# The out projection of a fused diffusion layer as seven block products per 256 tokens

## The chip, the cores and the metric

One core of one Trainium2 chip runs the whole program. The metric is the device time of one execution in microseconds; the median of three runs is given. Times inside the program come from one execution taken by the hardware profiler, counted from its first instruction.

## The reference, cut to what matters

The layer runs over 2,048 latent and 256 context tokens (2,304 in all) of 1,024 channels. Two branches (gated linear attention and a Fourier mixer) are each projected to 1,024 channels and merged by gates; what is changed is the last step:

```python
merged = jax.nn.sigmoid(mg_a) * y_a + jax.nn.sigmoid(mg_b) * y_b
x = x + gate[:, None] * (merged @ w_out)
...
y_prompt = _rmsnorm(hp, final_norm_g)
y_sample = _rmsnorm(hs, final_norm_g)
```

`merged` is 2304 x 1024, `w_out` is 1024 x 1024, and everything is float32. Each float32 product is made on TensorE from two roundings, `hi = round(x)` and `lo = x - hi`, as three matmuls: hi·hi, hi·lo and lo·hi.

## The kernel before, in words

The program is written for five engines by hand; every order is the order of the program text, and engines wait for each other's semaphores. The end of the program has three parts.

- **First branch's projection** (`second_branch`, 40 tiles) writes `meb_dram`.
- **Second branch's projection**: 40 tiles, tile `m` being output channels `j = m % 8` of token block `b = m // 8` (four blocks of 512 tokens and one of 256). Per tile TensorE makes 24 matmuls (L2554), DVE multiplies the bank by the gates (L2090), GpSimd adds the other branch (L1166), and SyncE stores the merged tile to `me_dram` (L948). SyncE is also the only queue for the loads.
- **Out projection** (`out_tiles`): nine blocks (`NM`) of `MB` = 256 tokens. A block is four output quarters (token half `u` by channel half `h`, 128 x 512 each) in four PSUM banks; a quarter is eight `k` steps of three matmuls of 512 columns (L2506 is the helper's line). So a block is 96 matmuls, and the nine are 864.

Around it, per block: one load `me_ld` of 1 MB (L970), its rounding on ScalarE (`me_hi`, L1504) and its remainder on DVE (`me_lo`, L1994), each one instruction over 128 x 2048; DVE scales each quarter by the gate row (L2114); GpSimd adds the residual `x_in` per 128 tokens, one instruction over 128 x 1024 (L1173, for the last block L1180); ScalarE squares and sums (L1583) and forms the root (L1585, L1587); DVE scales the rows (L2118; for the last block L2142 and L2147); SyncE stores. `w_out` is loaded in eight pieces, rounded by `high_ow` and finished by `low_ow` during the last blocks of the second branch. The gate rows are made once by two DVE adds (L2102).

## Time and profile before

| | us |
|---|---|
| median of three runs (1958.39 to 1962.95) | 1958.52 |
| span of the profiled execution, first to last instruction | 1959.3 |
| first to last matmul of the out projection | 1756.25 to 1952.34 |
| PE busy, whole span | 1914.4 |
| DVE, ACT, POOL busy, whole span | 1039.4, 876.2, 573.5 |

PE is TensorE's matmuls, PEld its weight loads, DVE is VectorE, ACT is ScalarE, POOL is GpSimd, SP is SyncE. The span of the profiled execution is 0.8 us above the median of the runs; no time outside the span is listed for it. A busy time of PE counts overlapping matmuls once. In the rows, "idle before" is the time that the engine stood still ahead of the instruction, with what released it.

### The profile page before, as it was taken

Reading aid. Unit: us, or ns where it says so; the run is one execution under the profiler, and the core shown is the slowest. Engines: PE = TensorE matmul, PEld = TensorE weight load, DVE = VectorE, ACT = ScalarE, POOL = GpSimd, SP = SyncE. Lnnn points to the kernel's source line nnn. Section 1 sums busy time; section 2 is a strip of 40 time slices with the busy share of each in tenths; the row PEclk is TensorE's granted clock in tenths of the full one; section 3 lists DMA queues with packets and bytes.
Section 4 is the critical chain, followed back from the end, with each engine's and each line's share of the span. In section 5 each row is a group of like instructions: output and inputs, shape, how many; then the busy total and the mean of one; then the engine's idle time right before and its main releaser. Section 6 shows DMA issues by size and latency. Waiting matters only on the chain.

```text
span 1959.3 us, 29951 instructions
## 1 busy us (share of the span) xinstructions
PE 1914.4 (98%) x10453; PEld 1763.4 (90%) x10453; DVE 1039.4 (53%) x1932; ACT 876.2 (45%) x1855; POOL 573.5 (29%) x645
## 2 busy tenths in 40 slices
PE   7899999999999999999999999999999999999998
PEld 2899999999999999999999987888888888898887
DVE  4978787784444435644444545666665322333333
ACT  3565667653445545443545325777732011112222
POOL 0136643053333412335432000002840033331122
PEclk9999999999999999999999999999999999999999
DMA  6578778967788889777888968666438666564333
GB/s 283 207 270 298 278 291 301 380 247 248 245 279 282 260 319 322 245 245 251 280 269 280 356 216 329 233 231 237 177 127 274 225 208 213 189 221 157 132 128 129
DMA packets 166827, 483.17 MB, mean 247 GB/s; under 512 B 14689, under 2 KB 51995, under 8 KB 157725
## 3 DMA queue, kind: packets, MB, share of 16 engines
q1 hardware_dynamic: 152860, 430.99, 63.7%
q10 hardware_dynamic: 13824, 50.34, 6.4%
q8 instruction: 83, 1.36, 0.3%
q14 instruction: 60, 0.48, 0.1%
HBM read 316.64 MB, written 155.20 MB: 241 GB/s over the span
## 4 chain that ended last, share of the span: by engine, by line
PE 72%; DMA 2%; DVE 2%; POOL 2%; ACT 1%; issue 1%; SPq 0%; DVEq 0%; ACTq 0%
PE bank L2219 34%; PE bank L2554 10%; PE bank L2506 10%; PE bank L2519 5%; PE bank L2383 3%; PE bank L2350 2%; PE bank L2448 2%; PE bank L2361 1%; PE bank L2372 1%; POOL h_lo L1038 1%; DMA qd<-qk_dec 1%; DMA x_st<-in_x 1%; PE bank L2391 1%; PE bank L2433 1%; DMA v_ld<-v_dram 1%
## 5 line engine op out<-in xcount | busy, mean ns | idle before, releaser
L2219 PE MATMUL bank<-h_hi,w_op 128*128 128x384 f32 x4032 | 1053.2, 337 | 14.3 <-DVE h_lo L1667 3.4
L2219 PEld LDWEIGHTS bank<-h_hi,w_op 128*128 128x128 f32 x4032 | 733.3, 189 | 20.1 <-issue 19.1
L2219 PE MATMUL bank<-h_lo,w_op 128*128 128x384 f32 x2016 | 675.9, 335 | 0.0
L2219 PEld LDWEIGHTS bank<-h_lo,w_op 128*128 128x128 f32 x2016 | 380.5, 189 | 0.0
L1661 DVE TENSOR_TENSOR w_op<-w_raw,w_op 128x512 fp32r<-128x512 f32 x240 | 190.0, 792 | 96.4 <-ACT w_op L1211 93.0
L1211 ACT ACTIVATE w_op<-w_raw 128x512 fp32r<-128x512 f32 x240 | 149.4, 624 | 160.4 <-PE bank L2219 155.9
L1063 POOL TENSOR_TENSOR decs<-decs,qk_s 128x192 f32<-128x192 f32 x192 | 123.7, 682 | 332.5 <-ACT decs L1285 332.2
L2554 PE MATMUL bank<-in_a,pwa 128*128 128x512 f32 (+1 forms) x960 | 197.3, 368 | 0.0
L2554 PEld LDWEIGHTS bank<-in_a,pwa 128*128 128x128 f32 x960 | 167.3, 189 | 30.0
L2506 PE MATMUL bank<-ow,me_hi 128*128 128x512 f32 x576 | 177.4, 389 | 0.0
L1716 DVE TENSOR_TENSOR outs<-bank,u 128x384 f32<-128x384 f32 x180 | 99.4, 552 | 100.4 <-PE bank L2219 99.5
L1166 POOL TENSOR_TENSOR me_st<-mg_a 128x512 f32<-128x512 f32 (+1 forms) x40 | 63.8, 1598 | 223.3 <-DVE mg_a L2090 223.3
L2506 PEld LDWEIGHTS bank<-ow,me_hi 128*128 128x128 f32 x576 | 107.9, 188 | 22.7 <-DVE me_lo L1994 0.2
L2506 PE MATMUL bank<-ow,me_lo 128*128 128x512 f32 x288 | 112.1, 389 | 0.0
L1048 POOL TENSOR_TENSOR swap<-swap,rope 128x192 f32<-128x192 f32 x96 | 61.1, 667 | 160.7 <-DMA swap<-qk_s 160.7
L1096 POOL TENSOR_TENSOR he<-uf 128x1023 f32<-128x1023 f32 (+2 forms) x7 | 18.7, 2666 | 285.4 <-DMA uf<-u_dram 285.4
L2519 PE MATMUL bank<-in_b,pwb 128*128 128x512 f32 (+1 forms) x480 | 99.3, 368 | 1.8 <-DVE in_b L1994 1.8
L2519 PEld LDWEIGHTS bank<-in_b,pwb 128*128 128x128 f32 x480 | 83.5, 189 | 17.5 <-DVE in_b L1994 2.7
L2090 DVE TENSOR_TENSOR mg_a<-bank,mg_a 128x512 f32<-128x512 f32 (+1 forms) x40 | 25.4, 637 | 136.8 <-PE bank L2554 136.8
L1716 DVE TENSOR_TENSOR u<-bank,p 128x384 f32<-128x384 f32 x72 | 39.9, 554 | 107.4 <-PE bank L2219 107.4
L2350 PE MATMUL bank<-v_ld,kin 128*128 128x256 f32 x272 | 83.3, 390 | 5.9 <-DMA v_ld<-v_dram 4.5
L1173 POOL TENSOR_TENSOR yt<-yt,x_in 128x1024 f32<-128x1024 f32 x16 | 38.1, 2398 | 140.0 <-DVE yt L2114 140.0
(244 smaller groups left out, 2622.2 us busy)
## 6 DMA issues: line engine op xcount, KB each, us to landing
w_op<-wt_dram SPq DMA_DIRECT2D x192, 512.0 KB, 5.6
wt_dram<-w_op ACTq DMA_DIRECT2D x96, 512.0 KB, 4.4
w_raw<-in_w_in SPq DMA_DIRECT2D x48, 768.0 KB, 6.1
w_raw<-in_w_in SPq DMA_DIRECT2D x24, 1024.0 KB, 6.7
qk_dec<-decs SPq DMA_DIRECT2D x48, 384.0 KB, 6.8
mg_dram<-outs SPq DMA_DIRECT2D x24, 768.0 KB, 6.9
swap<-qk_s SPq DMA_DIRECT2D x48, 192.0 KB, 5.8
v_dram<-outs SPq DMA_DIRECT2D x24, 384.0 KB, 4.7
```

Of the source, the lines that this page charges most:

```text
L1048: pool.tensor_tensor(swap[:, q], swap[:, q], rope[:, 1, q], ALU.mult)
L1063: ins = pool.tensor_tensor(e[:, q], e[:, q], qk_s[h % 2][:, x, q], ALU.mult)
L1166: pool.tensor_tensor(me_st[s][:, 0:n], mg_a[s][:, 0, 0:n], mg_a[s][:, 1, 0:n], ALU.add).then_inc(s_me, 1)
L1211: act.activation(w_op[m % RING][:, 0, :, :], w_part(n, j), ACT.Copy).then_inc(s_whi, 1)
L1661: dve.tensor_tensor(op[:, 1, :, :], w_part(n, j), op[:, 0, :, :].bitcast(F32), ALU.subtract).then_inc(s_wlo, 1)
L1716: dve.tensor_tensor(out, group_bank(n, g), other, ALU.add).then_inc(s_d, 1)
L2219: ins = pe.matmul(bnk, w_op[slot][:, part, k, :], h[:, j, k, :], start=(first and k == 0 and part == 0 and h is h_hi), stop=(k == HK - 1 a ...
L2350: pe.matmul(bank[4 + g % 2][:, 0:DV], kin[:, g % 2, :], v_ld[head % 2][:, chunk_at(head, x), :], start=True, stop=True).then_inc(s_ds, 1)
L2383: ins = pe.matmul(out, st, mv, start=False, stop=d == reads[-1])
L2506: ins = pe.matmul(out, st[a], mv[b], start=(k == 0 and p == 0), stop=(k == count - 1 and p == 2))
L2519: ins = pe.matmul(tile_bank(m)[:, 0:n], st[x], mv[y], start=(first and i == 0 and p == 0), stop=(final and i == len(ks) - 1 and p == 2))
L2554: ins = pe.matmul(out, pwa[j][x][:, k, :], in_a[b % 2][y][:, k, 0:n], start=(k == 0 and p == 0), stop=(k == KT - 1 and p == 2))
```

## The change

The 256-token product is made as a 2 x 2 block product with seven products instead of eight (Winograd's form of Strassen's scheme). With A the tokens' half by the channels' half (`a11` to `a22`, out of `me_ld`), and B the same of `w_out` (`b11`, `b21`, `b22`, `b12`):

- TensorE makes seven products of 4 `k` steps x 3 matmuls x 512 columns (`out_product`). Products 4, 5 and 6 add onto the banks of products 0, 2 and 3.
- Weights: `sum_ow` makes three sums and differences of the weight blocks (four instructions), and `high_ow` and `low_ow` now split seven operands of 128 x 2048 instead of eight of 128 x 1024. They stand in the second branch, from its third block to its last, and three `low_ow` stand behind it.
- Tokens: GpSimd makes four sums per block (`sum_me`, 128 x 512); ScalarE and DVE split seven operands of 128 x 512 each (`high_me`, `low_me`) in place of one of 128 x 2048.
- Results: ScalarE copies product 0 and one quarter out of PSUM (`copy_product`, `copy_quarter`); DVE makes five additions of 128 x 512 per block, each with one operand in PSUM (`add_quarter`). The scaling by the gate row moves from DVE to GpSimd, which now makes two instructions of 128 x 1024 per 128 tokens (`finish_rows`: multiply, then add the residual). The last block is finished in halves.
- The load of the gate rows, the norm's weights and the first `x_in` moves behind the last store of the merged tiles; the load of `pwa[7]` comes earlier. `yt` has two sets of buffers, the operands `me_op` have one. The block loop is written out instead of looped.

The diff, cut to its core (the placements in memory, the split of the last block of the second branch into `in_a_end`, and the final block's ScalarE part are left out; ACT copies from `out_bank(b, 0)`, `squares_of` is the old root code for 128 tokens, and the ACT order per block `b` is copy product 0, `squares_of(b - 1, 0)`, `high_me(b + 1, 0)`, `squares_of(b - 1, 1)`, `high_me` of operands 2, 1, 3 and 4, copy the quarter, `high_me` of 5 and 6):

```diff
             return bank[BANK_ORDER[n % 8]]
 
-        def out_bank(slot, u, h):
-            return bank[BANK_ORDER[4 * slot + 2 * u + h]]
+        def out_bank(b, g):
+            return bank[BANK_ORDER[4 * (b % 2) + g]][:, :]
+
+        def me_part(j):
+
+            a11, a12, a21, a22 = (me_ld[:, HK * c:HK * c + HK, P * r:P * r + P] for r in range(2) for c in range(2))
+            return (a11, me_s2[:, :, :], me_s1[:, :, :], a21, a12, me_s2[:, :, :], a22)[j]
+
+        def in_a_of(b, q):
+            return in_a_end[q] if b == NB - 1 else in_a[b % 2][q]
+
+        def in_a_raw_of(b):
+            return in_a_end_raw if b == NB - 1 else in_a_raw[b % 2]
+
+        FINAL = NM - 1
+        ME_ORDER = (0, 2, 1, 3, 4, 5, 6)
+        ME_MADE = (0, 2, 1, 3, 4, 5, 6)
+
+        def summed(b, n):
+
+            return 4 * NP + 4 * b + n + 1
+
+        def me_made(b, what):
+
+            return len(ME_MADE) * b + ME_MADE.index(what) + 1
+
 
...
+            def load_x(b, u):
+                sp.dma_start(x_in[:, u, :], io["x"][(2 * b + u) * P:(2 * b + u + 1) * P, :]).then_inc(s_xin[u], 16)
+
+            for r in range(2):
+                sp.dma_start(res_gate[:, r, :], gate_dram[r:r + 1].to_broadcast([P, D])).then_inc(s_rows, 16)
+            sp.dma_start(gate_b[:, :], io["b_gate"].to_broadcast([P, D])).then_inc(s_rows, 16)
+            sp.dma_start(fng[:, :], io["final_norm_g"].to_broadcast([P, D])).then_inc(s_rows, 16)
+            sp.wait_ge(s_y, 2 * NTILE)
+            for u in range(2):
+                load_x(0, u)
             for s in range(4):
                 sp.wait_ge(s_mest[s], 16 * (GATES_B[s] + NTILE // 4))
 
-            def out_block(b, final):
-
-                if not final:
-                    sp.wait_ge(s_ml, b + 1)
+            def store_y(b, u):
+                if b:
+                    sp.wait_ge(s_yst[u], 16 * b)
+                sp.wait_ge(s_yn, 2 * b + u + 1)
+                sp.dma_start(io["y"][(2 * b + u) * P:(2 * b + u + 1) * P, :], yt[b % 2][u][:, :]).then_inc(s_yst[u], 16)
+
+            for b in range(NM):
+                if b < FINAL:
+                    sp.wait_ge(s_ml, me_made(b, 6))
                     load_me(b + 1)
-                for u in range(2):
-                    if not final:
-                        sp.wait_ge(s_add, 2 * b + u + 1)
-                        sp.dma_start(x_in[:, u, :], io["x"][bass.ds((2 * b + u + 2) * P, P), :]).then_inc(s_xin[u], 16)
-                for u in range(2):
-                    if final and u:
-                        for h in range(2):
-                            sl = slice(512 * h, 512 * h + 512)
-                            sp.wait_ge(s_yn, 2 * b + 2 + h)
-                            sp.dma_start(io["y"][(2 * b + 1) * P:(2 * b + 2) * P, sl], yt[:, 1, sl]).then_inc(s_yst[1], 16)
-                        return
-                    sp.wait_ge(s_yn, 2 * b + u + 1)
-                    y = io["y"][bass.ds((2 * b + u) * P, P), :] if not final else io["y"][(2 * b + u) * P:(2 * b + u + 1) * P, :]
-                    sp.dma_start(y, yt[:, u, :]).then_inc(s_yst[u], 16)
...
+            def sum_me(b, n):
+
+                a11, a12, a21, a22 = (me_part(j) for j in (0, 4, 3, 6))
+                s1, s2 = me_s1[:, :, :], me_s2[:, :, :]
+                out, x, y, op = ((s1, a21, a22, ALU.add), (s2, s1, a11, ALU.subtract), (a21, a21, a11, ALU.subtract),
+                                 (s2, a12, s2, ALU.subtract))[n]
+                if n == 0:
+                    pool.wait_ge(s_mel, 16 * (b + 1))
+                    if b:
+                        pool.wait_ge(s_ml, me_made(b - 1, 6))
+                elif n == 3:
+                    pool.wait_ge(s_ml, me_made(b, 1))
+                else:
+                    pool.wait_ge(s_s, summed(b, 0))
+                pool.tensor_tensor(out, x, y, op).then_inc(s_s, 1)
+
             for m in range(NTILE):
                 b, j, t0, n = tile(m)
                 s = m % 4
@@ -1164,20 +1202,40 @@
                     pool.wait_ge(s_mest[s], 16 * (GATES_B[s] + m // 4))
                 pool.wait_ge(s_yg, NTILE + m + 1)
                 pool.tensor_tensor(me_st[s][:, 0:n], mg_a[s][:, 0, 0:n], mg_a[s][:, 1, 0:n], ALU.add).then_inc(s_me, 1)
-
-
-            def add_block(b):
+                if m == NTILE - 7:
+                    for i in range(3):
+                        sum_me(0, i)
+                elif m == NTILE - 3:
+                    sum_me(0, 3)
+
+
+            def finish_rows(b, u, sl, nth):
+
+                y = yt[b % 2][u][:, sl]
+                pool.tensor_tensor(y, y, res_gate[:, int(b == FINAL), sl], ALU.mult).then_inc(s_add, 1)
+                pool.wait_ge(s_add, nth)
+                pool.wait_ge(s_xin[u], 16 * (b + 1))
+                return pool.tensor_tensor(y, y, x_in[:, u, sl], ALU.add)
+
+            for n in range(3):
+                sum_me(1, n)
+            pool.wait_ge(s_gate, 1)
+            for b in range(FINAL):
+                sum_me(b + 1, 3)
                 for u in range(2):
-                    pool.wait_ge(s_xin[u], 16 * (b + 1))
-                    pool.wait_ge(s_og3, 2 * b + u + 1)
-                    pool.tensor_tensor(yt[:, u, :], yt[:, u, :], x_in[:, u, :], ALU.add).then_inc(s_add, 1)
-
-            with pool.Fori(0, NM // 2) as i:
-                for u in range(2):
-                    add_block(2 * i + u)
-            pool.wait_ge(s_xin[0], 16 * NM)
-            pool.wait_ge(s_og3, 2 * NM - 1)
-            pool.tensor_tensor(yt[:, 0, :], yt[:, 0, :], x_in[:, 0, :], ALU.add).then_inc(s_add, 1)
+                    if u == 0:
+                        pool.wait_ge(s_copied, 2 * b + 2)
+                    pool.wait_ge(s_ad, 5 * b + 4 + u)
+                    finish_rows(b, u, slice(0, D), 2 * (2 * b + u) + 1).then_inc(s_add, 1)
+                if b + 2 <= FINAL:
+                    for n in range(3):
+                        sum_me(b + 2, n)
+            pool.wait_ge(s_ad, 5 * FINAL + 3)
+            finish_rows(FINAL, 1, slice(512, D), 4 * FINAL + 1).then_inc(s_add, 1)
+            pool.wait_ge(s_copied, 2 * NM)
+            finish_rows(FINAL, 0, slice(0, 512), 4 * FINAL + 3).then_inc(s_add, 1)
+            pool.wait_ge(s_ad, 5 * FINAL + 4)
+            finish_rows(FINAL, 0, slice(512, D), 4 * FINAL + 5).then_inc(s_add, 1)
 
...
+            def high_ow(j):
+                if j in (1, 2, 3, 6):
+                    act.wait_ge(s_owl, {1: 3, 2: 1, 3: 2, 6: 4}[j])
+                if j in (0, 4, 5):
+                    act.wait_ge(s_wr[{0: 0, 4: 1, 5: 2}[j]], 48)
+                act.wait_ge(s_y, NTILE + 24 if j == 0 else NTILE + 32 + j)
+                act.activation(ow_op[j][0][:, :, :], ow_src[OW_PART[j]][:, :, :], ACT.Copy).then_inc(s_owh, 1)
+
+            def high_me(b, j):
+                act.wait_ge(s_mel, 16 * (b + 1))
+                if j in (1, 2, 3, 5):
+                    act.wait_ge(s_s, summed(b, {1: 1, 2: 0, 3: 2, 5: 3}[j]))
+                if b:
+                    act.wait_ge(s_out, NPROD * (b - 1) + j + 1)
+                elif j >= 5:
+                    act.wait_ge(s_y, 2 * NTILE)
+                act.activation(me_op[j][:, 0, :, :], me_part(j), ACT.Copy).then_inc(s_mh, 1)
 
             for b in range(NB):
...
+            def sum_ow(n):
+
+                b11, b21, b22, b12, t1, t2, t4 = (ow_src[name][:, :, :] for name in ("b11", "b21", "b22", "b12", "t1", "t2", "t4"))
+                out, x, y = ((t1, b12, b11), (b12, b12, b22), (t2, b22, t1), (t4, b21, t2))[n]
+                for k in ((3, 0), (2,), (), (1,))[n]:
+                    dve.wait_ge(s_wr[k], 48)
+                if n:
+                    dve.wait_ge(s_owl, n)
+                else:
+                    for s in range(GATE_SLOTS):
+                        dve.wait_ge(s_mest[s], 16 * GATES_B[s])
+                if n == 3:
+                    dve.wait_ge(s_y, NTILE + 24)
+                dve.tensor_tensor(out, x, y, ALU.subtract).then_inc(s_owl, 1)
+
+            def low_ow(j):
+                dve.wait_ge(s_owl, 4)
+                low(ow_op[j][1][:, :, :], ow_src[OW_PART[j]][:, :, :], ow_op[j][0][:, :, :], s_owh, j + 1, s_owl)
+
+            def low_me(b, j):
+                low(me_op[j][:, 1, :, :], me_part(j), me_op[j][:, 0, :, :], s_mh, NPROD * b + ME_ORDER.index(j) + 1, s_ml)
 
             for m in range(NTILE):
...
-                    low_ow(j - 4)
+                if b == 0 and j == 1:
+                    low(pwa[7][1][:, :, :], pwa_raw[7][:, :, :], pwa[7][0][:, :, :], s_pwh, 7 + 8, s_pwl)
+                if b == NB - 3 and j >= 5:
+                    sum_ow(j - 5)
+                elif b == NB - 2:
+                    if j == 0:
+                        sum_ow(3)
+                    elif j == 6:
+                        low_ow(0)
                 elif b == NB - 1:
                     if j == 1:
-                        low(me_lo[0][:, :, :], me_ld[:, :, :], me_hi[0][:, :, :], s_mh, 1, s_ml)
-                    elif 3 <= j < 7:
-                        low_ow(j + 1)
-            dve.wait_ge(s_rows, 16 * (8 + 4))
-            for r in range(2):
-                ins = dve.tensor_tensor(res_gate[:, r, :], res_gate[:, r, :], gate_b[:, :], ALU.add)
-            ins.then_inc(s_gate, 1)
-            dve.wait_ge(s_gate, 1)
...
+            def add_quarter(b, step):
+
+                y = yt[b % 2]
+                out, g, other, product = ((u2o[:, :], 1, p1o[:, :], 1), (u4o[:, :], 2, u2o[:, :], 2),
+                                          (y[1][:, 512:D], 3, u4o[:, :], 3), (y[0][:, 512:D], 2, u2o[:, :], 5),
+                                          (y[1][:, 0:512], 3, u2o[:, :], 6))[step]
+                if step == 0:
+                    dve.wait_ge(s_copied, 2 * b + 1)
+                if b + step:
+                    dve.wait_ge(s_ad, 5 * b + min(step, 2))
+                if step in (2, 3):
+                    if b > 1:
+                        dve.wait_ge(s_yst[1 if step == 2 else 0], 16 * (b - 1))
+                    elif b == 0:
+                        for s in range(4):
+                            dve.wait_ge(s_mest[s], 16 * (GATES_B[s] + NTILE // 4))
+                dve.wait_ge(s_out, NPROD * b + product + 1)
+                dve.tensor_tensor(out, out_bank(b, g), other, ALU.add).then_inc(s_ad, 1)
+
+            def scale_rows(b, u):
+                dve.wait_ge(s_rt3, 3 * (2 * b + u + 1) + (b == FINAL))
+                y = yt[b % 2][u][:, :]
+                dve.scalar_tensor_tensor(y, y, rms3[:, u, 1:2], fng[:, :], ALU.mult, ALU.mult).then_inc(s_yn, 1)
+
+            for b in range(NM):
+                if b:
+                    add_quarter(b - 1, 4)
+                    low_me(b, 6)
+                add_quarter(b, 0)
+                if b == 0:
+                    low_ow(5)
+                    low_me(0, 5)
+                    low_me(0, 6)
+                else:
+                    scale_rows(b - 1, 0)
+                add_quarter(b, 1)
+                if b == 0:
+                    low_ow(6)
+                    dve.wait_ge(s_rows, 16 * (8 + 4))
+                    for r in range(2):
+                        ins = dve.tensor_tensor(res_gate[:, r, :], res_gate[:, r, :], gate_b[:, :], ALU.add)
+                    ins.then_inc(s_gate, 1)
+                add_quarter(b, 2)
+                if b:
+                    scale_rows(b - 1, 1)
+                if b < FINAL:
+                    for j in (0, 2, 1):
+                        low_me(b + 1, j)
+                    for j in (3, 4):
+                        low_me(b + 1, j)
+                add_quarter(b, 3)
+                if b < FINAL:
+                    low_me(b + 1, 5)
+
+            sl, y = slice(0, 512), yt[FINAL % 2][1]
+            dve.wait_ge(s_ad, 5 * FINAL + 4)
+            dve.tensor_tensor(u4o[:, :], u2o[:, :], res_gate[:, 1, sl], ALU.mult).then_inc(s_ad, 1)
+            dve.wait_ge(s_ad, 5 * FINAL + 5)
+            dve.wait_ge(s_xin[1], 16 * NM)
+            dve.tensor_tensor(u4o[:, :], u4o[:, :], x_in[:, 1, sl], ALU.add).then_inc(s_ad, 1)
+            dve.wait_ge(s_ad, 5 * FINAL + 6)
+            dve.wait_ge(s_out, NPROD * NM)
+            dve.tensor_tensor(y[:, sl], out_bank(FINAL, 3), res_gate[:, 1, sl], ALU.mult).then_inc(s_ad, 1)
+            dve.wait_ge(s_ad, 5 * FINAL + 7)
+            dve.tensor_tensor(y[:, sl], y[:, sl], u4o[:, :], ALU.add).then_inc(s_ad, 1)
+            scale_rows(FINAL, 0)
+            dve.wait_ge(s_rt3, 6 * FINAL + 8)
             for h in range(2):
                 sl = slice(512 * h, 512 * h + 512)
-                ins = dve.tensor_tensor(yt[:, 0, sl], out_bank(0, 0, h)[:, :], res_gate[:, 1, sl], ALU.mult)
-            ins.then_inc(s_og3, 1)
-            dve.wait_ge(s_xin[1], 16 * NM)
-            scale_half(0)
...
+            def out_product(b, j):
+                bnk = out_bank(b, GROUP[j])
+                if b == 0:
+                    pe.wait_ge(s_owl, 4 + j + 1)
+                pe.wait_ge(s_ml, me_made(b, j))
+                if j < 4:
+                    if b < 2:
+                        pe.wait_ge(s_yg, 2 * NTILE - 8 + 4 * b + GROUP[j] + 1)
+                    elif j == 0:
+                        pe.wait_ge(s_copied, 2 * (b - 1))
+                    else:
+                        pe.wait_ge(s_ad, 5 * (b - 2) + (1, 4, 5)[j - 1])
+                elif j == 4:
+                    pe.wait_ge(s_copied, 2 * b + 1)
+                else:
+                    pe.wait_ge(s_ad, 5 * b + j - 3)
+                first = j < 4
+                for k in range(HK):
+                    for part, w in ((0, 0), (0, 1), (1, 0)):
+                        ins = pe.matmul(bnk, me_op[j][:, part, k, :], ow_op[j][w][:, k, :],
+                                        start=(first and k == 0 and part == w == 0), stop=(k == HK - 1 and part == 1),
+                                        skip_group_check=not first)
+                ins.then_inc(s_out, 1)
+
+            for b in range(NM):
+                for j in range(NPROD):
+                    out_product(b, j)
     return nc
 
```

## Rows read from the trace of the kernel before

**Rows 1.** The page: busy time of each engine, and the chain that ended last
```profile
PE 1914.4 (98%) x10453; PEld 1763.4 (90%) x10453; DVE 1039.4 (53%) x1932; ACT 876.2 (45%) x1855; POOL 573.5 (29%) x645
...
PE 72%; DMA 2%; DVE 2%; POOL 2%; ACT 1%; issue 1%; SPq 0%; DVEq 0%; ACTq 0%
PE bank L2219 34%; PE bank L2554 10%; PE bank L2506 10%; PE bank L2519 5%; PE bank L2383 3%; PE bank L2350 2%; PE bank L2448 2%; PE bank L2361 1%; PE bank L2372 1%; POOL h_lo L1038 1%; DMA qd<-qk_dec 1%; DMA x_st<-in_x 1%; PE bank L2391 1%; PE bank L2433 1%; DMA v_ld<-v_dram 1%
```

**Rows 2.** One stretch inside the out projection: window, length, busy us (instructions), clock, DMA
```profile
1900.00:1920.00 20.00, 20.00 (x90) 16.49 (x89) 7.58 (x7) 5.03 (x9) 4.76 (x2) 1.00 0.36 122
```

**Rows 3.** Timeline at the out projection's first and last matmuls and last DVE pair
```profile
1756.25 0.63 PE L2506 MATMUL bank<-ow,me_hi 128*128 128x512 f32 x2
...
1951.95 0.39 PE L2506 MATMUL bank<-ow,me_lo 128*128 128x512 f32 x1
...
1955.39 1.41 DVE L2147 SCALAR_TENSOR_TENSOR yt<-yt,rms,fng 128x512 f32<-128x512 f32 x2 [1.59 <-ACT rms L1571]
```

**Rows 4.** Groups by line and form from 1500 us on: busy us, mean ns, idle before
```profile
L1166 POOL TENSOR_TENSOR me_st<-mg_a 128x512 f32<-128x512 f32 x32 | 54.2, 1694 | 210.3 <-DVE mg_a L2090 210.3
...
L1994 DVE TENSOR_TENSOR me_lo<-me_ld,me_hi 128x2048 fp32r<-128x2048 f32 x9 | 20.6, 2292 | 85.6 <-ACT me_hi L1504 85.6
...
L1583 ACT ACTIVATE junk<-yt 128x1024 bf16<-128x1024 f32 x17 | 18.0, 1058 | 66.6 <-POOL yt L1173 58.2 <-POOL yt L1180 8.4
L1504 ACT ACTIVATE me_hi<-me_ld 128x2048 fp32r<-128x2048 f32 x9 | 17.2, 1917 | 127.9 <-DMA me_ld<-me_dram 127.9
...
L1585 ACT ACTIVATE rms<-rms 128x1 f32<-128x1 f32 x17 | 3.5, 203 | 0.5
...
L1994 DVE TENSOR_TENSOR in_a<-in_a_raw,in_a 128x512 fp32r<-128x512 f32 x4 | 2.7, 681 | 0.0
...
L1180 POOL TENSOR_TENSOR yt<-yt,x_in 128x1024 f32<-128x1024 f32 x1 | 2.4, 2388 | 7.8 <-DVE yt L2137 7.8
...
L1504 ACT ACTIVATE in_a<-in_a_raw 128x512 fp32r<-128x512 f32 x4 | 2.3, 624 | 21.7 <-DMA in_a_raw<-og_dram 21.7
...
L2128 DVE TENSOR_TENSOR yt<-bank,res_gate 128x512 f32<-128x512 f32 x2 | 1.4, 692 | 5.9 <-PE bank L2506 5.9
...
L2142 DVE SCALAR_TENSOR_TENSOR yt<-yt,rms,fng 128x1024 f32<-128x1024 f32 x1 | 1.3, 1278 | 0.0
```

**Rows 5.** GpSimd's and DVE's timelines in the second branch: start, length
```profile
1658.16 1.29 POOL L1166 TENSOR_TENSOR me_st<-mg_a 128x512 f32<-128x512 f32 x1 [4.15 <-DVE mg_a L2090]
1663.60 2.14 POOL L1166 TENSOR_TENSOR me_st<-mg_a 128x512 f32<-128x512 f32 x1 [4.15 <-DVE mg_a L2090]
...
1674.48 2.14 POOL L1166 TENSOR_TENSOR me_st<-mg_a 128x512 f32<-128x512 f32 x1 [3.30 <-DVE mg_a L2090]
...
1663.38 1.22 DVE L1994 TENSOR_TENSOR in_a<-in_a_raw,in_a 128x1024 fp32r<-128x1024 f32 x1
...
1675.39 2.32 DVE L1994 TENSOR_TENSOR ow<-ow_raw,ow 128x1024 fp32r<-128x1024 f32 x1
```

**Rows 6.** Timeline inside the out projection: DVE reading PSUM, GpSimd adding rows
```profile
1930.15 2.48 DVE L2114 TENSOR_TENSOR yt<-bank,res_gate 128x512 f32<-128x512 f32 x4
...
1931.51 4.77 POOL L1173 TENSOR_TENSOR yt<-yt,x_in 128x1024 f32<-128x1024 f32 x2 [17.13 <-DVE yt L2114]
...
1935.74 1.62 DVE L2118 SCALAR_TENSOR_TENSOR yt<-yt,rms,fng 128x1024 f32<-128x1024 f32 x1 [3.11 <-ACT rms L1587]
```

**Rows 7.** DMA issues from 1600 us on: KB each, median us to landing
```profile
me_ld<-me_dram SPq DMA_DIRECT2D x9, 1024.0 KB, 7.7
x_in<-in_x SPq DMA_DIRECT2D x18, 512.0 KB, 3.5
```

**Rows 8.** Timeline at the first block: last merged stores, the adds of the gate rows, second load
```profile
1761.98 2.36 DVE L2102 TENSOR_TENSOR res_gate<-res_gate,gate_b 128x1024 f32<-128x1024 f32 x2 [4.69 <-DMA res_gate<-gate_dram]
...
1758.09 1.03 SPq L948 DMA_DIRECT2D me_dram<-me_st  x2
1766.32 0.42 SPq L970 DMA_DIRECT2D me_ld<-me_dram  x1
```

284 lines of the change are left out of this document (135 added, 149 removed).

## The prediction

> **What bounds the kernel now.** I read the page first. TensorE is busy 98% of the span and carries 72% of the chain that ended last; the out projection's line, L2506, is 10% of it [rows 1]. A share says nothing about one stage, so next I took the table by windows. In twenty microseconds of the out projection TensorE has no gap at full clock, while DVE works 7.6, ScalarE 5.0 and GpSimd 4.8 us [rows 2]. The timeline gives the stage: first matmul at 1756.25, last one ending at 1951.95 + 0.39 = 1952.34, so 196.1 us for 864 matmuls, 0.227 us each, and 21.8 us per block of 96. DVE's last instruction ends at 1956.80, 4.5 us behind TensorE, and the span 2.5 us after that [rows 3]. The stage is bound by TensorE, and the change takes an eighth of it: 108 matmuls x 0.227 = 24.5 us, leaving 84 x 0.227 = 19.1 us per block. The question is what the other engines do in 19.1 us.
>
> **The port that GpSimd and DVE share.** The durations that I need are GpSimd 1.29 us for 128x512 and 2.39 for 128x1024; DVE 0.68 for a 128x512 remainder, 0.69 with one operand in PSUM, 2.29 for 128x2048, 1.28 for a row scaling of 128x1024; ScalarE 0.62 for a 128x512 rounding, 1.06 for the squares and 0.20 for each step of the root [rows 4, 5]. But GpSimd's 128x512 addition has a mean of 1.69, and the timeline shows why. It takes 1.29 while DVE is idle (at 1658.16). At 1663.60 it takes 2.14: DVE's remainder, both operands in SBUF, runs from 1663.38 to 1664.60, and 1663.60 + 2.14 - 1.29 = 1664.45, so GpSimd did nothing until 0.15 before DVE's end. The reverse too: at 1675.39 DVE's instruction takes 2.32 instead of 1.22, starting work at 1676.49, 0.13 before GpSimd's end at 1676.62 [rows 5]. So these instructions exclude each other whole. DVE reading PSUM does not take part: four such instructions take 2.48 with GpSimd beginning at 1931.51 among them, and GpSimd's pair takes 4.77 = 2 x 2.39 undisturbed. The row scaling does: 1.62 instead of 1.28 [rows 4, 6]. The Trainium skill, "SBUF — State Buffer", section "Who interferes with whom", says the same (a DVE instruction with two SBUF inputs and a GpSimd instruction that reads SBUF hold one lock) and thereby speaks against work for GpSimd here. Its section "A bandwidth-pool intuition that's wrong" puts the blocked side's restart at about 115 ns behind DVE's end, measured there on descriptors; the rows have it 0.15 ahead. With that figure GpSimd's five waits below would be 0.27 longer each, an estimate of some 1.3 us per block.
>
> **The loop of the new block.** Per block GpSimd has four sums and four instructions of 1024: 4 x 1.29 + 4 x 2.39 = 14.7 us. DVE's exclusive part is seven remainders (4.8) and two scalings (2.6), 22 us together on one port against TensorE's 19.1; only what overlaps in waiting for nothing saves them. I follow the chain round, from one `sum_me(b+1, 0)` to the next, in program order:
> - sums 0, 1 and 2: 3.9, and 1.0 of waiting, since `scale_rows(b-1, 1)` takes the port between sums 1 and 2;
> - sum 3 waits for `low_me(b+1, 1)`, which on DVE stands behind that scaling and behind `low_me` 0 and 2. Those can begin only when sum 2 has gone: three of 0.6 plus 0.1 = 1.9. Then 0.3 behind `low_me` 3, and 1.3;
> - `finish_rows(b, 0)` waits for `add_quarter(b, 3)`, behind `low_me` 4, which itself waited for sum 3: 1.3;
> - four instructions of 2.39 = 9.6, with waits behind `low_me` 5 (0.3), `low_me` 6 (0.3) and `scale_rows(b, 0)` (0.9); own semaphores 0.2.
> Sum: 3.9 + 1.0 + 1.9 + 0.3 + 1.3 + 1.3 + 9.6 + 1.5 + 0.2 = 21.0; carried to hundredths it is 20.9. TensorE sits inside it: product 0 of a block needs `low_me(b+1, 0)`, which comes late by the difference. So a block costs 20.9 us instead of 21.8, not 19.1. DVE and ScalarE are not bounds: DVE's 10.8 us (five additions too) and ScalarE's 8.5 leave room.
>
> **The start.** In the second branch four `sum_ow` and most of the seven `high_ow` and `low_ow` (2.3 each, up to twice that beside GpSimd) lie on DVE between tiles of 3 to 5 us and beside TensorE, which has eight banks of slack; I price them at nothing, and if that cover fails it is one 2.3 us each. What remains is behind the last tile: `low_ow(3)` and `low_ow(4)` hold up GpSimd's last merged tile to about 5 us after the first product begins, against 1.9 now; four row loads and two x loads, which stood ahead of it, now come behind. Now the second `me_ld` is issued 10.1 us after the stage's start, and the gate rows are there 5.7 us after it [rows 3, 8]. I put that load at 13 us, landing at 20 (7 of the 5.5 to 7.7 us that such loads show [rows 7]), and the gate rows at 14, for which product 6 of block 0 waits 0.8. So `sum_me(1, 0)` begins at 20. The first round is a little shorter (no rows to finish before its sums): 19.7. Then seven rounds of 20.9: 20.0 + 19.7 + 146.3 = 186.0, the point at which GpSimd turns to the last block's rows.
>
> **The end.** Now GpSimd is free before the last product; the last DVE work ends 4.5 us behind TensorE. In the change six GpSimd instructions of 1.29 remain at 186.0, when TensorE has still 3.8 us to go. The first takes 1.3, then x (issued as the queue's last load, 3.5 us [rows 7]) is waited for until 190.3; five more with 1.4 us of port waits: 198.1. Then squares 1.4, root 0.5, the other half's squares 0.8, sum 0.3, root 0.5, two scalings of 0.75: 202.9. Now it is 1956.80 - 1756.25 = 200.6. The changed stage is therefore 2.3 us longer, although its matmuls end at about 189.8 instead of 196.1: that gain is given back in the tail. The profiled span 1959.3 becomes 1961.6; it stood 0.8 above the median of the runs, so 1958.5 + 2.3 = 1960.8, and I say 1961. What is moved or added elsewhere (load of `pwa[7]`, `w_out` in four pieces of 1 MB a block earlier) lies beside tiles whose loads run four ahead: nothing, at worst 3 us if a merge load is late.
>
> **Bounds.** A port wait removed altogether takes 2.9 us out of a round; below 19.1 TensorE bounds. All of DVE's exclusive work unhidden gives 22.1. Eight rounds between 19.1 and 22.1 are -14 to +10 us about the forecast, and the tail moves with them.
>
> **The rivals.**
> - *TensorE keeps the stage.* If the port costs little, blocks run at 19.1, GpSimd (14.7 of 19.1) keeps up, the tail stays 7.0: 1958.5 - 24.5 = 1934, with one late gate row 1936. For it: DVE and GpSimd together work 12.3 of 20 us now [rows 2]. Against: the exclusion is exact in rows 5 and 6. 0.08.
> - *GpSimd bounds, but waits fall better.* DVE may get through in gaps in which I let it meet GpSimd; at 19.9 a round and a tail 2 us shorter, 1961 - 8 - 2 = 1951, and between 1940 and 1952.6 altogether. 0.17.
> - *The block's load lands late* (slower). `me_ld` of the next block is issued when `low_me(b, 6)` is done, 8.0 us before GpSimd wants it. Landing takes 7.7 in the middle now [rows 7], with x loads in between. From 8.0 on each further microsecond lengthens every one of seven rounds: 9 us gives +7 and +2 at the start, 1970. For it: 0.3 us of slack by that median; against: the stores that lengthen it now are farther off. 0.13. Port waits longer than mine, by the skill's restart for one, would end in the same range, some 10 us up at 1971. 0.09.
> - *The forecast*, within 6 us of no change: 0.53.
>
> **How the numbers follow.** The three runs lie within 0.25%, so 0.3%, 5.9 us, is about what can be told from no change. Faster than 1952.6: 0.08 + 0.17 = 0.25. Slower than 1964.4: 0.13 + 0.09 = 0.22. Same: 0.53. The range leaves out the first rival and the best of the second below 1945 (0.12) and above 1970 half of the slower cases' far end (0.08).
>
> **What would show it.** Right: 756 matmuls in the stage; blocks about 20.9 apart, with TensorE idle 1.6 us ahead of each product 0, released by `low_me`; GpSimd over 80% busy (14.7 + 2.9 of 20.9) in the stage and its 128x1024 means above 2.39, `sum_me` means near 1.6; the end of the last matmul near 190 us after the stage's start and a tail of over 13 us led by GpSimd. Wrong: `sum_me` at 1.29 throughout (first rival), ScalarE or GpSimd waiting for `me_ld` in each block (third), or idle TensorE in the second branch, which I priced at nothing.

## The result, and the profile after

| | before | after |
|---|---|---|
| median of 20 runs, us | 1959.01 (1953.75 to 1965.06) | 1963.81 (1957.86 to 1966.29) |
| span of the profiled execution, us | 1959.3 | 1959.2 |
| out projection: first matmul to the end of DVE's last instruction | 1756.25 to 1956.80 = 200.6 | 1750.89 to 1956.41 = 205.5 |

The ratio of after to before is 1.0021, with a 95% interval of 1.0012 to 1.0030: 4.1 us longer (2.4 to 5.9; the two medians are 4.8 apart), inside the 0.3% that was called no change. The median of 1963.81 lies 0.6 us below the upper edge of that, 1964.4. The two spans hide this. The profiled execution of after came to the out projection 5.4 us earlier than that of before, and the same 5.4 us were there already at the first matmul with `in_b` (1452.7 against 1458.1), ahead of everything that the change adds; then it lost 5.0 us in the stage. So stages are compared here, not spans.

The page of the changed kernel: busy times, the chain that ended last, and the costliest group of the out projection (busy, mean ns, idle time before).

```profile
PE 1891.4 (97%) x10345; PEld 1740.1 (89%) x10345; DVE 1113.1 (57%) x1999; ACT 909.0 (46%) x1926; POOL 693.4 (35%) x702
...
PE 77%; POOL 7%; DVE 6%; DMA 5%; ACT 2%; issue 2%; SPq 1%; ACTq 0%; POOLq 0%; DVEq 0%
...
L2746 PE MATMUL bank<-ow_op,me_op 128*128 128x512 f32 x756 | 177.9, 394 | 15.8 <-DVE me_op L2104 9.1
```

TensorE works 23 us less than before and has 108 matmuls fewer [rows 1], but GpSimd and DVE have 13% of the chain between them where they had 4%. Now TensorE stands still for 15.8 us inside the stage. Its timeline shows where:

```profile
1750.89 16.51 PE L2746 MATMUL bank<-ow_op,me_op 128*128 128x512 f32 x72
1772.30 7.27 PE L2746 MATMUL bank<-ow_op,me_op 128*128 128x512 f32 x24 [4.90 <-DVE yt L2263]
1779.95 11.17 PE L2746 MATMUL bank<-ow_op,me_op 128*128 128x512 f32 x48 [0.38 <-DVE me_op L2104]
1792.93 5.72 PE L2746 MATMUL bank<-ow_op,me_op 128*128 128x512 f32 x24 [1.80 <-DVE u4o L2263]
1799.86 19.60 PE L2746 MATMUL bank<-ow_op,me_op 128*128 128x512 f32 x84 [1.21 <-DVE me_op L2104]
...
1841.57 19.64 PE L2746 MATMUL bank<-ow_op,me_op 128*128 128x512 f32 x84 [1.24 <-DVE me_op L2104]
1862.44 19.60 PE L2746 MATMUL bank<-ow_op,me_op 128*128 128x512 f32 x84 [1.23 <-DVE me_op L2104]
...
1924.99 19.60 PE L2746 MATMUL bank<-ow_op,me_op 128*128 128x512 f32 x84 [1.27 <-DVE me_op L2104]
```

There are three irregular waits at the start, and then one of 1.2 us ahead of each block's first product. The first wait also costs speed behind it: the granted clock was 1.00 up to 1771 us, 0.50 from 1772 to 1775 (1.2 instead of 2.4 GHz) and 1.00 again from 1776, and the 24 matmuls took 7.27 us instead of 24 x 0.227 = 5.4. From 1799.86 to 1924.99 a block takes 20.86 us; before it took 21.8. The last matmul ends at 1944.59, 193.7 us after the stage's start (196.1 before), and DVE's end comes 11.8 us behind it (4.5 before). Here is one round on GpSimd. L1196 is `sum_me`; L1215 and L1218 are the multiplication and the addition of `finish_rows`.

```profile
1836.09 1.29 POOL L1196 TENSOR_TENSOR me_s<-me_ld 128x512 f32<-128x512 f32 x1
1837.46 1.30 POOL L1196 TENSOR_TENSOR me_s<-me_s,me_ld 128x512 f32<-128x512 f32 x1
1838.70 2.26 POOL L1196 TENSOR_TENSOR me_ld<-me_ld 128x512 f32<-128x512 f32 x1
1842.80 1.68 POOL L1196 TENSOR_TENSOR me_s<-me_ld,me_s 128x512 f32<-128x512 f32 x1 [1.83 <-DVE me_op L2104]
1845.77 2.72 POOL L1215 TENSOR_TENSOR yt<-yt,res_gate 128x1024 f32<-128x1024 f32 x1 [1.29 <-DVE yt L2263]
1848.57 2.73 POOL L1218 TENSOR_TENSOR yt<-yt,x_in 128x1024 f32<-128x1024 f32 x1
1851.26 2.39 POOL L1215 TENSOR_TENSOR yt<-yt,res_gate 128x1024 f32<-128x1024 f32 x1
1853.73 3.26 POOL L1218 TENSOR_TENSOR yt<-yt,x_in 128x1024 f32<-128x1024 f32 x1
1856.95 1.30 POOL L1196 TENSOR_TENSOR me_s<-me_ld 128x512 f32<-128x512 f32 x1
```

And DVE in the same round: L2268 is `scale_rows`, L2104 is `low_me`, L2263 is `add_quarter`, whose other operand is a PSUM bank.

```profile
1837.81 2.02 DVE L2268 SCALAR_TENSOR_TENSOR yt<-yt,rms,fng 128x1024 f32<-128x1024 f32 x1 [2.62 <-ACT rms L1656]
1839.76 1.76 DVE L2104 TENSOR_TENSOR me_op<-me_ld,me_op 128x512 fp32r<-128x512 f32 x1
1841.44 1.28 DVE L2104 TENSOR_TENSOR me_op<-me_s,me_op 128x512 fp32r<-128x512 f32 x2
1842.64 2.38 DVE L2104 TENSOR_TENSOR me_op<-me_ld,me_op 128x512 fp32r<-128x512 f32 x2
1844.95 0.68 DVE L2263 TENSOR_TENSOR yt<-bank,u2o 128x512 f32<-128x512 f32 x1
1845.55 0.68 DVE L2104 TENSOR_TENSOR me_op<-me_s,me_op 128x512 fp32r<-128x512 f32 x1
```

Read the two as one port. GpSimd's third sum is recorded from 1838.70 for 2.26 us, of which 1.29 is work, so it began to work at 1839.67, 0.16 before DVE's scaling ended (1837.81 + 2.02 = 1839.83). DVE's next remainder, recorded from 1839.76, ends at 1841.52, 0.56 after GpSimd's sum did (1840.96), instead of 0.68. Then GpSimd waits 1.83 us for three remainders in a row, and 1.29 for an addition. The port rests only from 1845.02 to 1845.55, while DVE works out of PSUM: it is held for 20.3 of 20.86 us. The instructions of a block need 22.0 us at their undisturbed durations, and they fit because recorded durations overlap: by 0.13 to 0.21 us where the port changes sides, and by 0.08 between two DVE instructions in a row (1.28 for two of 0.68). The lock that the Trainium skill describes ("SBUF — State Buffer", section "Who interferes with whom") is seen again in these rows.

The means of the stage say the same: 2.99 and 2.56 for an instruction of 2.39 (L1218, L1215), 2.32 and 1.64 for the third and the fourth sum of 1.29, and 1.81 for a scaling of 1.28.

```profile
L1218 POOL TENSOR_TENSOR yt<-yt,x_in 128x1024 f32<-128x1024 f32 x16 | 47.9, 2993 | 1.3
L1215 POOL TENSOR_TENSOR yt<-yt,res_gate 128x1024 f32<-128x1024 f32 x16 | 40.9, 2557 | 10.9 <-DVE yt L2263 10.9
L2268 DVE SCALAR_TENSOR_TENSOR yt<-yt,rms,fng 128x1024 f32<-128x1024 f32 x17 | 30.7, 1807 | 53.0 <-ACT rms L1656 53.0
...
L1196 POOL TENSOR_TENSOR me_ld<-me_ld 128x512 f32<-128x512 f32 x9 | 20.9, 2322 | 0.0
...
L1196 POOL TENSOR_TENSOR me_s<-me_ld,me_s 128x512 f32<-128x512 f32 x9 | 14.7, 1637 | 13.5 <-DVE me_op L2104 13.5
```

The start of the stage, from the timelines of DVE, SP's queue, ScalarE and GpSimd (L1204 is the last merged tile, L2286 the additions of the gate rows, L986 the second `me_ld`):

```profile
1756.79 2.27 DVE L2104 TENSOR_TENSOR ow_op<-ow_b,ow_op 128x2048 fp32r<-128x2048 f32 x1
...
1757.02 2.65 POOL L1204 TENSOR_TENSOR me_st<-mg_a 128x256 f32<-128x256 f32 x1 [2.63 <-DVE mg_a L2219]
...
1760.06 0.93 SPq L992 DMA_DIRECT2D res_gate<-gate_dram  x2
...
1763.45 23.45 SPq L986 DMA_DIRECT2D me_ld<-me_dram  x2
...
1769.20 2.36 DVE L2286 TENSOR_TENSOR res_gate<-res_gate,gate_b 128x1024 f32<-128x1024 f32 x2 [3.33 <-DMA fng<-in_final_norm_g]
1771.47 0.68 DVE L2263 TENSOR_TENSOR yt<-bank,u4o 128x512 f32<-128x512 f32 x1
...
1774.62 0.63 ACT L1603 ACTIVATE me_op<-me_ld 128x512 fp32r<-128x512 f32 x1 [19.67 <-DMA me_ld<-me_dram]
```

DVE's remainder of a weight block holds GpSimd off the last merged tile (2.65 instead of 0.74). Its store, behind it the rows' loads at 1760.06, and behind these x and the second `me_ld` (the first of the two issued in that row) follow on one queue. The rows are there at 1769.20, `me_ld` 11.2 us after its issue. Over all nine loads of `me_ld` the trace has the line below; in the seven rounds ScalarE takes the load up 5.1 to 5.4 us after its issue.

```profile
DMA to landing us min/median/max: 5.0/5.1/11.2
```

The end, GpSimd's and DVE's timelines:

```profile
1940.35 1.29 POOL L1215 TENSOR_TENSOR yt<-yt,res_gate 128x512 f32<-128x512 f32 x1
1944.50 1.29 POOL L1218 TENSOR_TENSOR yt<-yt,x_in 128x512 f32<-128x512 f32 x1 [2.87 <-DMA x_in<-in_x]
...
1950.44 1.26 POOL L1218 TENSOR_TENSOR yt<-yt,x_in 128x512 f32<-128x512 f32 x1
...
1955.00 1.41 DVE L2315 SCALAR_TENSOR_TENSOR yt<-yt,rms,fng 128x512 f32<-128x512 f32 x2 [0.33 <-ACT rms L1656]
```

### The profile page after: what moved, and what is told of

It is laid out like the page before. It is cut to its first block, busy times and chain, and to the rows that moved or that the text cites. A ratio compares the mean times of both kernels' runs of the same rounds, so it can differ in the third digit from the quotient of the medians.

```text
span 1959.2 us, 29859 instructions
## 1 busy us (share of the span) xinstructions
PE 1891.4 (97%) x10345; PEld 1740.1 (89%) x10345; DVE 1113.1 (57%) x1999; ACT 909.0 (46%) x1926; POOL 693.4 (35%) x702
## 4 chain that ended last, share of the span: by engine, by line
PE 77%; POOL 7%; DVE 6%; DMA 5%; ACT 2%; issue 2%; SPq 1%; ACTq 0%; POOLq 0%; DVEq 0%
PE bank L2387 46%; PE bank L2722 10%; PE bank L2687 5%; PE bank L2551 3%; POOL yt L1218 3%; PE bank L2518 2%; POOL yt L1215 2%; DVE me_op L2104 2%; DMA x_st<-in_x 2%; PE bank L2616 2%; PE bank L2529 1%; PE bank L2540 1%; POOL h_lo L1060 1%; PE bank L2331 1%; DMA qd<-qk_dec 1%
## 5 line engine op out<-in xcount | busy, mean ns | idle before, releaser
L2746 PE MATMUL bank<-ow_op,me_op 128*128 128x512 f32 x756 | 177.9, 394 | 15.8 <-DVE me_op L2104 9.1
L2746 PEld LDWEIGHTS bank<-ow_op,me_op 128*128 128x128 f32 x756 | 141.4, 189 | 52.0 <-DVE me_op L2104 12.8
L2722 PE MATMUL bank<-in_a,pwa 128*128 128x512 f32 x768 | 174.3, 389 | 0.0
L2722 PEld LDWEIGHTS bank<-in_a,pwa 128*128 128x128 f32 x768 | 144.1, 188 | 29.9
L1204 POOL TENSOR_TENSOR me_st<-mg_a 128x512 f32<-128x512 f32 (+1 forms) x40 | 72.3, 1809 | 210.5 <-DVE mg_a L2219 210.5
L1826 DVE TENSOR_TENSOR u<-bank,u 128x384 f32<-128x384 f32 x72 | 39.9, 555 | 67.6 <-PE bank L2387 67.2
L1293 ACT ACTIVATE p<-bank 128x384 f32<-128x384 f32 x72 | 35.2, 489 | 89.5 <-PE bank L2387 89.5
```

The costliest lines, as they stand in the source:

```text
L1204: pool.tensor_tensor(me_st[s][:, 0:n], mg_a[s][:, 0, 0:n], mg_a[s][:, 1, 0:n], ALU.add).then_inc(s_me, 1)
L1826: dve.tensor_tensor(out, group_bank(n, g), other, ALU.add).then_inc(s_d, 1)
L2722: ins = pe.matmul(out, pwa[j][x][:, k, :], in_a_of(b, y)[:, k, 0:n], start=(k == 0 and p == 0), stop=(k == KT - 1 and p == 2))
L2746: ins = pe.matmul(bnk, me_op[j][:, part, k, :], ow_op[j][w][:, k, :], start=(first and k == 0 and part == w == 0), stop=(k == HK - 1 and p ...
```

## The experiments

All are edits of the changed kernel, and each ratio is to the kernel before (with its 95% interval, from 4 to 10 runs of the edit). "Stage" is measured as in the table above. "Round" is the distance between the first matmuls of two blocks in the middle (where TensorE has no gap, 84 matmuls at its mean pace). "Port work" counts a block's exclusive instructions at their undisturbed durations [rows 4, 5]: for the changed kernel 4 x 1.29 + 4 x 2.39 on GpSimd and 7 x 0.68 + 2 x 1.28 on DVE, 22.0 us.

| kernel | port work | round | stage | ratio |
|---|---|---|---|---|
| before | | 21.8 | 200.6 | 1 |
| after | 22.0 | 20.86 | 205.5 | 1.0021 (1.0012 to 1.0030) |
| e1, no gate multiplication | 17.3 | 19.1 | 185.7 | 0.9925 (0.9910 to 0.9941) |
| e2, scaling on ScalarE | 19.5 | 19.8 | 194.6 | 0.9968 (0.9956 to 0.9980) |
| e3, sums on DVE | 19.6 | 19.1 | 190.7 | 0.9938 (0.9925 to 0.9952) |
| e4, second load first | 22.0 | 20.86 | 203.3 | 1.0008 (0.9999 to 1.0018) |
| e5, gate multiplication on DVE | 19.7 | 19.9 | 195.6 | 0.9979 (0.9961 to 0.9998) |
| e6, sums and start | 19.6 | 19.1 | 181.1 | 0.9887 (0.9870 to 0.9903) |
| e7, sums, start and end | 19.6 | 19.1 | 178.2 | 0.9872 (0.9854 to 0.9891) |

**e1: is it GpSimd and its port at all?** The multiplication by the gate row is left out in all blocks but the last.

```diff
-                pool.tensor_tensor(y, y, res_gate[:, int(b == FINAL), sl], ALU.mult).then_inc(s_add, 1)
-                pool.wait_ge(s_add, nth)
+                if b == FINAL:
+                    pool.tensor_tensor(y, y, res_gate[:, 1, sl], ALU.mult).then_inc(s_add, 1)
+                    pool.wait_ge(s_add, nth)
```

> Leaves out the multiplication by the gate row in the first eight blocks (GpSimd's 128x1024 multiply, 2.4 us twice a block); the last block is complete. Theory (GpSimd, with its waits for the shared port, sets the round of 20.85 us): its work falls from 14.7 to 9.9 us a block, so TensorE sets the round again, 19.1 to 19.6 us, TensorE has hardly a gap ahead of product 0, and the stage (first out projection matmul to the end of the last DVE instruction, 205.5 us in the changed kernel) falls to 186 to 191. Rival A (the load of the next block's tokens, or the order of DVE's remainders, sets the round): the round stays within 0.3 of 20.85, since neither has changed.

TensorE's timeline has one group without a gap from the third block on:

```profile
1800.03 133.62 PE L2747 MATMUL bank<-ow_op,me_op 128*128 128x512 f32 x588 [0.72 <-DVE me_op L2105]
```

133.62 / 588 = 0.227 us for one: the stage was not bound by TensorE, and it is as soon as 4.8 us of GpSimd's work are gone. This takes the same 4.8 us off the port, so e1 doesn't part the two. The stage ended just below its expected range. The start keeps its gaps (3.53 us the largest).

**e2: GpSimd's own work, or the port?** The scaling by the norm goes from DVE to ScalarE, and GpSimd's program stays as it is.

```diff
+                if b:
+                    for u in range(2):
+                        act.wait_ge(s_rt3, 3 * (2 * (b - 1) + u + 1))
+                        rows_of = yt[(b - 1) % 2][u][:, :]
+                        act.activation(rows_of, rows_of, ACT.Copy, scale=rms3[:, u, 1:2]).then_inc(s_yn, 1)
...
-                    scale_rows(b - 1, 0)
...
-                    scale_rows(b - 1, 1)
```

> Moves the row scaling of the first eight blocks from DVE (two operands in SBUF) to ScalarE, which leaves out the multiplication by the final norm's weight there; GpSimd's instructions are all kept. Theory (waits for the shared port are part of the round): the two waits of 0.9 and 1.0 us behind the scalings vanish, the second 128x1024 addition falls from 3.26 to about 2.4 us and the mean of that group from 2.99 to below 2.65; the round falls to 19.7 to 20.2 us and the stage to 197 to 202. Rival B (GpSimd's own 14.7 us and its turn-taking with DVE by semaphores set the round, the port is beside the point): instruction lengths stay, round 20.6 to 20.9. Rival A: round 20.85.

A group of GpSimd, TensorE's timeline, and a row of GpSimd's in the round behind it:

```profile
L1218 POOL TENSOR_TENSOR yt<-yt,x_in 128x1024 f32<-128x1024 f32 x16 | 40.9, 2559 | 1.3
```

```profile
1862.77 19.37 PE L2747 MATMUL bank<-ow_op,me_op 128*128 128x512 f32 x84 [0.34 <-DVE me_op L2109]
...
1877.21 1.30 POOL L1196 TENSOR_TENSOR me_s<-me_ld 128x512 f32<-128x512 f32 x1 [0.69 <-DMA me_ld<-me_dram]
```

The mean of the addition falls from 2.99 to 2.56 without a change to GpSimd (the second one of a round from 3.26 to 2.39), the wait ahead of product 0 from 1.24 to 0.34, the round by 1.1. So it is the shared port and not GpSimd by itself. How much of the 1.1 us is the port alone is not shown: the largest single gain is GpSimd's wait ahead of the fourth sum, 0.62 instead of 1.83, and the remainders that it waits for also no longer stand behind a scaling in DVE's own order. The stage ended 2.4 us below its expected range. Two waits are new or longer: GpSimd waits 0.69 for `me_ld`, which it never did in a round of the changed kernel, and 1.94 instead of 1.29 ahead of its first multiplication, now for ScalarE's `copy_quarter`, which stands behind the two scalings.

**e3: the token sums on the other side of the port.** `sum_me` moves from GpSimd to DVE, where a remainder of the same size takes 0.68 instead of 1.29.

```diff
                 add_quarter(b, 2)
+                if b < FINAL:
+                    for n in range(3):
+                        sum_me(b + 1, n)
                 if b:
                     scale_rows(b - 1, 1)
                 if b < FINAL:
                     for j in (0, 2, 1):
                         low_me(b + 1, j)
+                    sum_me(b + 1, 3)
```

> Nothing is left out: the four token sums of a block move from GpSimd to DVE (0.7 us each in place of 1.3), three of them ahead of the scaling of the second rows. Theory: port time per block falls from 22 to 19.7 us, and GpSimd's chain from 14.7 to 9.6 with no handshake between sums and remainders; TensorE sets the round, 19.1 to 19.4, stage 191 to 194, about 12 us less than the changed kernel and 6 to 9 less than the kernel before: ratio to before 0.995 to 0.997. Rival B (GpSimd's own work is what counts): the same round, so this run doesn't part the two. Rival C (DVE becomes the bound, since 13.6 us of work and every port wait now fall on it): round 20 or more. Rival A: round 20.85.

TensorE's timeline:

```profile
1777.27 4.37 PE L2742 MATMUL bank<-ow_op,me_op 128*128 128x512 f32 x12 [4.88 <-DVE yt L2255]
1782.34 152.62 PE L2742 MATMUL bank<-ow_op,me_op 128*128 128x512 f32 x672 [0.70 <-DVE me_op L2077]
```

From the second block on TensorE has no gap, and the kernel beats the one before by 0.6%, better than expected. e2 and e3 have the same port work, 19.5 and 19.6 us, and rounds of 19.8 and 19.1. So the sum of the port's work is not all. The reading that fits is that with the sums on DVE one engine runs through sums and remainders in its own order, and GpSimd stands outside that chain; it is argued and not isolated, since e2 also has its waits for the load and for ScalarE.

**e4: the start alone, the load.** The second `me_ld` is issued ahead of the two x loads.

```diff
-            for u in range(2):
-                load_x(0, u)
             for s in range(4):
                 sp.wait_ge(s_mest[s], 16 * (GATES_B[s] + NTILE // 4))
+            sp.wait_ge(s_ml, me_made(0, 6))
+            load_me(1)
+            for u in range(2):
+                load_x(0, u)
```

> The load of the second block's tokens is issued ahead of the two loads of x instead of behind them. Theory (that load landed 11.2 us after its issue because 3 MB stood in front of it): with 2 MB in front it lands some 3 us earlier, GpSimd's first sum of block 1 begins 3 us earlier, rounds stay 20.85, stage 202 to 203. Rival (the start is set by the gate rows and DVE's queue of weight remainders): stage within 0.5 of 205.5.

```profile
1779.19 23.88 PE L2748 MATMUL bank<-ow_op,me_op 128*128 128x512 f32 x96 [4.91 <-DVE yt L2265]
1804.30 19.62 PE L2748 MATMUL bank<-ow_op,me_op 128*128 128x512 f32 x84 [1.24 <-DVE me_op L2106]
```

The waits of 0.38 and 1.80 us in TensorE's timeline are gone, and the stage is 2.2 us shorter. The wait of 4.9 us is not: it belongs to the gate rows, not to the load. Rounds stay at 20.86. The load, with 2 MB ahead of it, is taken up 9.0 us after its issue (1770.08 to 1779.09), not 3 but 2.2 us sooner than with 3 MB, and the stage is 0.3 us above its expected range. The interval of this ratio overlaps that of the change, so the 2.2 us rest on the two traces.

**e5: the multiplication on DVE.** The sums stay on GpSimd; DVE multiplies by the gate row, at 1.22 instead of 2.39.

```diff
+            def gate_rows(b, u):
+                if u == 0:
+                    dve.wait_ge(s_copied, 2 * b + 2)
+                dve.wait_ge(s_ad, 5 * b + 4 + u)
+                y = yt[b % 2][u][:, :]
+                dve.tensor_tensor(y, y, res_gate[:, 0, :], ALU.mult).then_inc(s_owh, 1)
...
                     low_me(b, 6)
+                    gate_rows(b - 1, 1)
...
                     low_me(b + 1, 5)
+                    gate_rows(b, 0)
```

> Nothing is left out: in the first eight blocks DVE multiplies by the gate row (128x1024, both operands in SBUF, 1.22 us twice a block) and GpSimd keeps the token sums and the residual addition. Theory (port time and GpSimd's chain): GpSimd falls to 9.9 us a block, DVE rises to 13.2, 9.8 of it on the port, 19.7 us of port time in all as with the sums moved; but the multiplies stand in DVE's queue ahead of additions that TensorE waits for: round 19.8 to 20.2, stage 195 to 199, ratio to before 0.997 to 0.999. Rival B (GpSimd's own work alone): 19.1 and a stage of 187 to 190, as when the multiplication is left out. Rival C (DVE is the bound now): above 20.5.

GpSimd's timeline in one round, and the load's issue on SP's queue:

```profile
1859.87 1.67 POOL L1196 TENSOR_TENSOR me_s<-me_ld,me_s 128x512 f32<-128x512 f32 x1 [1.83 <-DVE me_op L2107]
...
1873.04 1.29 POOL L1196 TENSOR_TENSOR me_s<-me_ld 128x512 f32<-128x512 f32 x1 [1.66 <-DMA me_ld<-me_dram]
```

```profile
1867.64 0.38 SPq L986 DMA_DIRECT2D me_ld<-me_dram  x1
```

The port work is that of e3 again, and the round is 19.9. The wait of 1.83 us ahead of the fourth sum is that of the changed kernel to the hundredth, and the first sum now waits 1.66 us for the load, which landed 5.4 us after its issue (1867.64 to 1873.04). GpSimd also waits 3.14 and 1.92 us a round for DVE's multiplications. TensorE in turn waits 0.5 to 0.7 us a block for an addition (`u4o`) that stands behind a scaling of 3.18 us instead of 1.28. Which of these waits keeps e5 at 19.9, and which of its own keeps e2 at 19.8, was not taken apart: no run had a second place for `me_ld`.

**e6: sums on DVE and a mended start.** e3 and e4 together; besides, the gate rows and the norm's weights are loaded two and one merged tiles earlier, and two weight blocks are split ahead of the first tokens, which wait for their load.

```diff
+                if m == NTILE - 3:
+                    for r in range(2):
+                        sp.dma_start(res_gate[:, r, :], gate_dram[r:r + 1].to_broadcast([P, D])).then_inc(s_rows, 16)
+                elif m == NTILE - 2:
+                    sp.dma_start(fng[:, :], io["final_norm_g"].to_broadcast([P, D])).then_inc(s_rows, 16)
...
-                    high_me(0, 0)
                     high_ow(1)
+                    high_ow(2)
+                    high_me(0, 0)
```

> Nothing is left out. On top of the token sums on DVE: the second block's tokens are loaded ahead of x, three of the four row loads are issued behind the 38th and 39th merged tile instead of behind the 40th, and ScalarE and DVE split the weight operands 1 and 2 before the first tokens. Theory (the start's 6.6 us of TensorE gaps come from one queue of loads and from DVE's late weight remainders, which waited behind the first tokens' load): gaps shrink to 1 to 3 us, stage from 190.7 to 185 to 187. Rival (DVE's own work before the first third addition is the limit, 8 instructions of 2.3 us): gaps stay above 5 us, stage 189 or more.

```profile
1755.31 171.55 PE L2745 MATMUL bank<-ow_op,me_op 128*128 128x512 f32 x756
```

All 756 matmuls run in one group without a gap, at 0.227 us each; one to three us of gaps had been expected, and a stage of 185 to 187 instead of 181.1. Against e3 the stage is 9.6 us shorter: 6.6 are e3's gaps, some 1.9 are matmuls of e3's at the lower clock behind its long wait (granted 0.50 from 1777 to 1780 us, 12 matmuls in 4.37 us instead of 2.7), and 0.8 lie in the tail behind the last matmul (10.3 and 9.6 us). Which of the start's edits did it was not taken apart.

**e7: the end too.** The last block's x goes into `me_ld`'s place, which is free early, and DVE finishes the quarter of `y[0]` that GpSimd had.

```diff
+                if b == FINAL:
+                    sp.wait_ge(s_ml, me_made(b, 6))
+                    for u in range(2):
+                        sp.dma_start(x_end[:, u, :], io["x"][(2 * b + u) * P:(2 * b + u + 1) * P, :]).then_inc(s_pbr[u], 16)
...
-            pool.wait_ge(s_ad, 5 * FINAL + 4)
-            finish_rows(FINAL, 0, slice(512, D), 4 * FINAL + 5).then_inc(s_add, 1)
```

> Nothing is left out. On top of that, the last block's x is loaded to a place of its own as soon as the last tokens are split, and DVE makes the two steps of one of the three GpSimd halves at the end. Theory (the tail behind the last matmul, 10.3 us with the sums on DVE, is 3 us of waiting for x and 6 GpSimd instructions in a row): tail 5 to 7 us, stage 180 to 183, ratio to before 0.989 to 0.992. Rival (the tail is set by the squares, root and scaling chain behind the last addition): tail within 1 us of 10.3.

```profile
1915.60 1.29 POOL L1204 TENSOR_TENSOR yt<-yt,res_gate 128x512 f32<-128x512 f32 x1
1916.96 1.29 POOL L1207 TENSOR_TENSOR yt<-yt,x_end 128x512 f32<-128x512 f32 x1
...
1927.80 1.41 DVE L2324 SCALAR_TENSOR_TENSOR yt<-yt,rms,fng 128x512 f32<-128x512 f32 x2 [0.33 <-ACT rms L1637]
```

The addition of x follows its multiplication at once, where 2.87 us of waiting stood before; TensorE's last matmul ends at 1922.55, DVE at 1929.21: a tail of 6.7 us, instead of 9.6 in e6 and 11.8 in the changed kernel. The stage and the ratio are better than expected (178.2 against 180 to 183, 0.9872 against 0.989 to 0.992). The intervals of e6 and e7 overlap, so the 2.9 us between their stages rest on the two traces. This kernel beats the one before by 1.3% (median 1934.67 against 1959.68), with all of the change's arithmetic in it.

## Why the forecast held, and where its sum was off

In us from the first matmul of the stage:

| step of the sum | forecast | measured |
|---|---|---|
| `sum_me(1, 0)` begins | 20.0 | 1774.67 - 1750.89 = 23.8 |
| first round on GpSimd | 19.7 | 1794.39 - 1774.67 = 19.7 |
| seven rounds | 146.3 | 1940.35 - 1794.39 = 146.0 |
| from there to DVE's end | 16.9 | 1956.41 - 1940.35 = 16.1 |
| stage | 202.9 | 205.5 |
| longer than before | 2.3 | 5.0 in the two traces, 4.1 by the ratio of the runs |

**The loop was right, in size and in its parts.** Forecast were waits of 1.0, 1.9 + 0.3, 1.3 and 1.5 on GpSimd; the round shown above has 0.97, 1.83 + 0.39, 1.29 and 1.54 (0.33 + 0.34 + 0.87). A block costs 20.86 where 20.9 was forecast. That the port lengthens GpSimd's instructions, and that GpSimd's work alone does not set the round, is shown by e2, and that TensorE would otherwise keep 19.1 by e1, e3 and e6. The wait ahead of product 0 is 1.24, forecast as 1.6; the rest of 20.86 - 19.06 = 1.8 lies in smaller waits inside the block. What the forecast did not say is that the port is full, 20.3 of 20.86 us: it read a chain that went back and forth. Here both readings give the same round; e2, e3 and e5, with the same port work and rounds of 19.8, 19.1 and 19.9, speak for the chain. The restart of 115 ns behind DVE's end that the Trainium skill gives ("SBUF — State Buffer", section "A bandwidth-pool intuition that's wrong") would have made a block some 1.3 us longer, an estimate from that page; the measured 20.86 and the restart 0.16 ahead of the end decide against it for these instructions; the page's figure was measured on descriptors.

**The failed step is "The start".** Its term, 20.0 for `sum_me(1, 0)`, measured 23.8. Issuing was as forecast (12.6 against 13), although the last merged tile came 3.8 us later than forecast; landing took 11.2 us instead of 7 (the kernel before has 5.5 to 8.3, median 7.7). Ahead of the load, four row loads and two x loads of 0.5 MB each, 3 MB, had gone out within 3.4 us; the median of rows 7 was taken in rounds in which this does not occur. e4 puts the load first and takes 2.2 us back. In the same step the gate rows were put at 14 and were there at 18.3, because the last merged tile was finished at 8.8 (1759.67), not at 5: DVE's remainders of weights hold the port and the queue, 1.9 us of it directly. So the weights' splits are not free. Inside the second branch they are, as priced: TensorE has no gap there, and both kernels take 298.2 us from the first matmul with `in_b` to the stage. What DVE has left of them behind it costs more than forecast. ScalarE takes `high_me(0, 0)` first, which waits for its load until 1738.67, and all splits of weights stand behind it. TensorE waits 4.90 us ahead of product 6, forecast as 0.8. What that wait alone costs in the changed kernel was not isolated, since GpSimd's chain sets the pace there; where TensorE sets it, as in e3 and e6, all waits at the start together, with the slower matmuls behind them, cost 8.8 of the 9.6 us between these two.

**The end** was 0.8 shorter than forecast, and led by GpSimd, with a wait of 2.87 for x and port waits; the tail behind the last matmul is 11.8 instead of 13.1, because the last matmul itself came 3.9 later. e7 takes out the late x and one of GpSimd's last halves, and the tail falls from 9.6 us (e6) to 6.7; the rest of it was not tested. The terms of this step as written add up to 203.1, 0.2 more than the 202.9 that was carried on; nothing hangs on it.

**The rivals.** TensorE does not keep the stage with this order of work. The waits do not fall better: none of them is shorter than forecast by more than 0.1. The block's load lands late only at the start. In the rounds it is issued 7.9 us before GpSimd wants it, as forecast (8.0), and it lands in 5.0 to 5.4 us, not in 7.7, so it has at least 2.5 us of slack and not 0.3; it becomes a wait for GpSimd only when the round gets shorter (e1, e2, e5). ScalarE does wait for it in every round, 1.2 to 1.5 us, which the prediction had named as a sign that it was wrong. This costs nothing: ScalarE rounds that operand at 1833.62, and DVE takes it up only at 1839.76. The slack and the loop's fit are why the slower cases did not come. That the change ended within 0.3%, although its sum missed half of the difference, is partly luck: the median lies 0.6 us inside that margin, and the start was 3.8 us longer than forecast against 0.8 us gained in the end.

## What to carry to other kernels

When an algorithm takes products off TensorE, price what it adds on the port that GpSimd and DVE share, instruction by instruction in the program order of both, before counting the matmuls saved: here 22 us of exclusive work (20.3 with its overlaps) stood against 19.1 us of matmuls, and moving four sums to the faster side of the same port turned +0.2% into -0.6%. Then look at the two ends of the stage, where a gain in the loop is easily given back: the order of loads on one queue, small rows that everything waits for, and the last block's x were worth nearly as much here (-0.6% to -1.3%). A duration from issue to landing holds only for the queue in which it was measured.

## What the runs showed of the hardware that was not expected

- The same load of 1 MB landed 11.2 us after its issue behind 3 MB of other loads, 9.0 behind 2 MB (e4), and 5.0 to 5.4 in the changed kernel's rounds.
- Behind a wait of 4.9 us TensorE's granted clock was 0.50 for some 3 us (1772 to 1775 in the changed kernel, 1777 to 1780 in e3), and 1.00 a microsecond before and a microsecond behind that. Such a gap costs more than itself where TensorE sets the pace.
- The hand-over of the port is within 0.2 us: the blocked side began 0.16 before the other's recorded end (1839.67 against 1839.83), and 0.13 at the last merged tile (1757.02 + 2.65 - 0.74 = 1758.93 against 1756.79 + 2.27 = 1759.06). None of the rows shown has a restart behind that end.
- The change and e4 run the same program up to the out projection and come to it 6.9 us apart (1750.89 and 1757.77), more than the change's whole effect. The mean granted clock of the two executions was 0.992 and 0.989; how much of the 6.9 us that makes was not taken apart. One profile each does not carry a comparison of spans here.
